# A two-block network on one core: filter spectra in four parts at four token norms, a second filter in the hyena output, two `w_out` pieces on VectorE, two `oa` chunks behind the inverse

## The reference, cut to what matters

```python
# once per layer; depends on the weights alone, not on the tokens
h = sin(freq[0] * (z @ fw1 + fb1)); h = sin(freq[1] * (h @ fw2 + fb2)); h = sin(freq[2] * (h @ fw3 + fb3))
h = (h @ fw4).reshape(L, 2, 512) * decay[:, None, :]
k = concat([h_fwd, 0, h_bwd[:0:-1]])
v_f, k_f = rfft(v, n=2 * L), rfft(k, n=2 * L)      # v depends on the tokens
y = irfft(v_f * k_f)[:, :L] + v * bias             # then times x0, then w_o_hyena
```

## Time and profile before

| | |
|---|---|
| runs of before, median of 3 | 2634.07 us (2632.21 to 2635.34) |
| the profiled execution | 2638.58 us, span 2636.6 us |
| PE matmul busy | 2520.5 us, 96% of the span |
| DVE, ACT, POOL busy | 43%, 48%, 55% |
| chain that ended last | PE 87%, ACT 5%, DVE 4%, issue 1%, POOL 1%, DMA 1% |
| mean granted TensorE clock | 0.986 |

### The profile page before, as it was taken

How to read it: one execution, slowest core, us unless ns; L and a number is a source line. 1 busy time by engine, 2 the same in 40 slices (tenths; PEclk the granted TensorE clock), 3 DMA queues, 4 the chain that set the end, 5 groups by cost and what they waited for, 6 DMA issues and landing times.

```text
span 2636.6 us, 42005 instructions
## 1 busy us (share of the span) xinstructions
PE 2520.5 (96%) x16564; PEld 2170.2 (82%) x16564; DVE 1131.5 (43%) x2158; ACT 1276.9 (48%) x2118; POOL 1440.5 (55%) x829
## 2 busy tenths in 40 slices
PE   6999999998999899999799999989999989999997
PEld 6998889988999789987577766766888868888997
DVE  7785545443976554534315512132101123525323
ACT  5457954355447964444544411342333345536543
POOL 5875746447976655444533122753555546463970
PEclk9999999999999999999899999999999999999999
DMA  5543343344543453343421111231222233234553
GB/s 217 191 161 145 128 160 145 130 178 173 191 161 144 144 177 112 144 152 141 160 80 65 49 64 64 96 116 72 90 94 96 96 112 112 86 136 180 189 180 143
DMA packets 50551, 347.62 MB, mean 132 GB/s; under 512 B 5312, under 2 KB 8640, under 8 KB 8896
## 3 DMA queue, kind: packets, MB, share of 16 engines
q1 hardware_dynamic: 47840, 340.31, 35.6%
q10 hardware_dynamic: 2528, 4.72, 0.5%
HBM read 343.96 MB, written 1.05 MB: 131 GB/s over the span
## 4 chain that ended last, share of the span: by engine, by line
PE 87%; ACT 5%; DVE 4%; issue 1%; POOL 1%; DMA 1%; SPq 0%; ACTq 0%; POOLq 0%; DVEq 0%
PE pg L1873 22%; PE pg L1875 21%; PE pg L1874 21%; PE pg L1898 2%; PE ps L2166 2%; PE ps L2187 2%; PE ps L2185 1%; PE pg L1896 1%; ACT ring_hi L758 1%; PE ps L2324 1%; PE ps L2305 1%; PE ps L1996 1%; PE ps L2021 1%; DMA ring<-in_w_stream_dram 1%; PE ps L2015 1%
## 5 line engine op out<-in xcount | busy, mean ns | idle before, releaser
L649 POOL TENSOR_TENSOR ring_lo<-ring,ring_hi 128x1024 fp32r<-128x1024 f32 (+2 forms) x498 | 1154.7, 2333 | 768.3 <-ACT ring_hi L758 767.9
L1873 PE MATMUL pg<-HH,ring_hi 128*128 128x256 f32 (+1 forms) x3360 | 1084.4, 323 | 45.3 <-DVE HL L1322 16.0
L1874 PE MATMUL pg<-HH,ring_lo 128*128 128x256 f32 (+1 forms) x3360 | 1029.9, 307 | 0.0
L1875 PE MATMUL pg<-HL,ring_hi 128*128 128x256 f32 (+1 forms) x3104 | 957.3, 308 | 0.0
L1873 PEld LDWEIGHTS pg<-HH,ring_hi 128*128 128x128 f32 x3360 | 641.3, 191 | 132.3 <-issue 64.2
L1874 PEld LDWEIGHTS pg<-HH,ring_lo 128*128 128x128 f32 x3360 | 642.3, 191 | 45.6 <-issue 18.2
L1875 PEld LDWEIGHTS pg<-HL,ring_hi 128*128 128x128 f32 x3104 | 592.9, 191 | 30.6
L758 ACT ACTIVATE ring_hi<-ring 128x1024 fp32r<-128x1024 f32 (+6 forms) x564 | 555.1, 1002 | 36.3 <-DMA ring<-in_w_stream_dram 35.4
L768 ACT ACTIVATE take<-pg 128x256 f32<-128x256 f32 (+1 forms) x260 | 110.9, 426 | 506.3 <-PE pg L1875 457.1
L1875 PE MATMUL pg<-big_r,ring_hi 128*128 128x256 f32 (+1 forms) x864 | 274.7, 318 | 0.0
L1873 PE MATMUL pg<-big_r,ring_hi 128*128 128x256 f32 (+1 forms) x736 | 240.3, 326 | 7.1 <-DVE big_r L1810 3.1
(11 more groups left out here) (327 smaller groups left out, 3214.5 us busy)
## 6 DMA issues: line engine op xcount, KB each, us to landing
ring<-in_w_stream_dram SPq DMA_DIRECT2D x320, 1024.0 KB, 4.8
hn<-in_consts_dram ACTq DMA_DIRECT2D x2, 1024.0 KB, 5.7
cst<-in_consts_dram SPq DMA_DIRECT2D x1, 1472.0 KB, 19.8
prm<-in_params_dram SPq DMA_DIRECT2D x1, 1110.0 KB, 7.4
X<-in_xT_dram SPq DMA_DIRECT2D x1, 1024.0 KB, 5.8
X<-in_ctxT_dram ACTq DMA_DIRECT2D x1, 1024.0 KB, 6.5
out_dram<-H ACTq DMA_DIRECT2D x1, 1024.0 KB, 4.8
cst<-in_consts_dram SPq DMA_DIRECT2D x1, 768.0 KB, 16.7
```

The source lines that it names most:

```text
L649: pool.tensor_tensor(ring_lo[:, slot, cols], ring[:, slot, cols], ring_hi[:, place * P:(place + n) * P].bitcast(F32), SUB).then_inc(sem(LO ...
L1873: first = pe.matmul(out, a[0], b[0], start=start, stop=False)
L1874: pe.matmul(out, a[1], b[0], start=False, stop=False)
L1875: return first, pe.matmul(out, a[0], b[1], start=False, stop=stop)
```

## The change

The spectrum is cut into four parts of 4 matmuls (8 instructions) each, every one into one bank: 2 or 3 of `ps`. Layer 0's parts stand at norms 2 and 3, layer 1's at norms 4 and 5: one part before the wait for the norm's sum (in place of the half `mod` chunk, which moves behind the sum with the other half), one part after the `mod` chunk. ACT copies the parts out two and two: parts 0 and 1 of layer 0 behind the squares of norm 3, all others behind the modulation (`modulate`) that follows. On DVE, layer 1's sine arguments and decay stand before the low parts of `mg2` 0, 1, 3 and 4; on PE, its steps stand behind `oh` 1, 4, 7 and 10. Layer 1's steps 0 to 3 move from the feed-forward into layer 0's `oh` chunks, with their table loads. The piece of `w_out` 1 goes to DVE and out of the hold. One turn (`modt`) moves one chunk later. In layer 1, two `oa` chunks move behind the inverse transform.

```diff
-    return gates[:2] + [row] + gates[2:3] + [turn] + gates[3:]
+    return gates[:2] + [row] + gates[2:4] + [turn] + gates[4:]
...
-    return spread([("oa", l, i) for i in range(2 * KD)], 5 if l == 0 else 3)
+    outs = [("oa", l, i) for i in range(2 * KD)]
+    return spread(outs, 5) + [[]] if l == 0 else spread(outs[:-2], 3) + [outs[-2:]]
...
-    if name == "w_out" and i == 0:
+    if name == "w_out" and i < 2:
         return True
...
-            need = [piece[4] for piece in PIECES if piece[8] <= last + (group[0][0] == "d_out")]
+            need = [piece[4] for piece in PIECES if piece[8] <= last + 2 * (group[0][0] == "d_out")]
...
+        KF_BANKS = (2, 3)
+        SPECTRA = {2: ([(0, 0)], [(0, 1)]), 3: ([(0, 2)], [(0, 3)]), 4: ([(1, 0)], [(1, 1)]), 5: ([(1, 2)], [(1, 3)])}
...
-        FILTER_1 = [6, 12, 3, 9, 13]
-        FILTER_2 = [0, 1, 2, 3, 4]
+        FILTER_1 = [6, 12, 3, 9]
+        FILTER_2 = [1, 4, 7, 10]
+        DECAY_AT = [0, 1, 3, 4]
...
+            def filter_spectrum(l, parts):
+                for ft in parts:
+                    act.wait_ge(sem("kf_ready"), 4 * l + ft + 1)
+                    act.activation(KFT[:, ft, :], ps[:, KF_BANKS[ft % 2], :], ACT.Copy).then_inc(sem("kf_done"), 1)
...
             for m in range(KD):
                 norm_square(3, m)
+            filter_spectrum(0, (0, 1))
             drain_fill(norm_mods(2, "turns"))
             norm_root(3)
...
                 modulate(mix_norm[l], l, 0)
+                filter_spectrum(l, (2, 3))
...
                 for i in range(2 * KD):
+                    if l == 0 and i - 2 in FILTER_2[:3]:
+                        ahead(CHUNK["oh", l, i])
+                        filter_sin(1, FILTER_2.index(i - 2))
                     drain_fill([("oh", l, i)])
+                    if l == 0 and i == 0:
+                        act.wait_ge(sem("hyena"), N_SEQ[0])
+                        act.dma_start(W4[0:64, :], fw4[1]).then_inc(sem("w4_loaded"), 16)
+                        act.dma_start(hn[:, :], consts[:, N_KEPT:]).then_inc(sem("filter_tables"), 16)
...
                 modulate(ffn_norm[l], l, 1)
                 if l == 0:
-                    act.wait_ge(sem("hyena"), N_SEQ[0])
-                    act.dma_start(W4[0:64, :], fw4[1]).then_inc(sem("w4_loaded"), 16)
-                    act.dma_start(hn[:, :], consts[:, N_KEPT:]).then_inc(sem("filter_tables"), 16)
+                    filter_spectrum(1, (0, 1))
...
+                    elif m in DECAY_AT[:3]:
+                        filter_argument(1, DECAY_AT.index(m))
+                    elif m == DECAY_AT[3]:
+                        filter_decay(1)
...
+            def filter_spectrum(l, ft):
+                bank = KF_BANKS[ft % 2]
+                if ft == 0:
                     pe.wait_ge(sem("h4_done"), l + 1)
+                if ft >= 2:
+                    pe.wait_ge(sem("kf_done"), 4 * l + ft - 1)
+                for q in range(4):
+                    ins = pe.matmul(ps[:, bank, :], table[...], VTK[:, q, :], start=q == 0, stop=q == 3)
+                ins.then_inc(sem("kf_ready"), 1)
...
             def norm(i):
-                fill(norm_mods(i, "before"))
+                if i in SPECTRA:
+                    for l, ft in SPECTRA[i][0]:
+                        filter_spectrum(l, ft)
+                else:
+                    fill(norm_mods(i, "before"))
                 pe.wait_ge(sem("norm_sum"), i + 1)
                 pe.matmul(ps[:, 0, 0:n], ones, rstd[:, 0:n], start=True, stop=True).then_inc(sem("norm_ss"), 1)
                 fill(norm_mods(i, "after"))
+                if i in SPECTRA:
+                    for l, ft in SPECTRA[i][1]:
+                        filter_spectrum(l, ft)
...
+                for i in range(1, 2 * KD):
+                    fill([("oh", l, i)])
+                    if l == 0 and i in FILTER_2:
+                        filter_step(1, FILTER_2.index(i))
```

More of the change, by code:

```diff
@@ L896, in filter_sin @@
                 act.activation(HQ[0:64, :], RR[0:64, 0, :], ACT.Sin).then_inc(sem("f_sin"), 1)
-            def filter_spectrum(l):
-                act.wait_ge(sem("kf_ready"), l + 1)
-                act.activation(KFT, ps[:, :, :], ACT.Copy).then_inc(sem("kf_done"), 1)
+            def filter_spectrum(l, parts):
+                for ft in parts:
+                    act.wait_ge(sem("kf_ready"), 4 * l + ft + 1)
+                    act.activation(KFT[:, ft, :], ps[:, KF_BANKS[ft % 2], :], ACT.Copy).then_inc(sem("kf_done"), 1)
             def attention_exp(l, it):
@@ L1094, in _ @@
                         filter_sin(0, 1 if m == 0 else 2)
-                    if l == DEPTH - 1 and m == KD - 1:
-                        merged_high(m - 1)
-                        ahead(CHUNK["d_out", l, 2 * m + 1])
-                        filter_spectrum(0)
                     drain_fill([("d_out", l, 2 * m + 1)])
-                    if 0 < m < KD - 1 or m and l < DEPTH - 1:
+                    if m:
                         merged_high(m - 1)
@@ L1184, in _ @@
                 drain_fill(next(gaps))
-                for s in range(ns):
-                    drain_fill(next(gaps))
-                    if s < ns - 1:
-                        drain_fill(next(gaps))
+                for items in gaps:
+                    drain_fill(items)
                 def merged2_high(m):
@@ L1211, in _ @@
                     drain(CHUNK["gu", l, 2 * i], AF[l][:, i % per, :], ACT.Silu, n)
-                    if l == 0 and i in FILTER_2[1:4]:
-                        filter_sin(1, FILTER_2.index(i) - 1)
                     to_take("gu", l, 2 * i + 1, n=n)
@@ L1218, in _ @@
                         hidden_high(i - 1)
-                    if l == 0 and i == FILTER_2[4] + 1:
-                        filter_spectrum(1)
                     if i % per == per - 1:
@@ L1793, in _ @@
                     dve.wait_ge(sem("vf_ready"), k + 1)
-                    dve.wait_ge(sem("kf_done"), l + 1)
+                    dve.wait_ge(sem("kf_done"), 4 * (l + 1))
                     dve.tensor_tensor(YFT[:, re, :], VFT[:, re, :], KFT[:, re, :], MUL)
@@ L1821, in _ @@
                     modulation(1, 0)
-                    for k in range(3):
-                        filter_argument(1, k)
-                    filter_decay(1)
                 for i in range(KF):
@@ L1976, in filter_step @@
                             pe.wait_ge(sem("hn_done"), HN_BASE1(1) + DO_N + 1)
-                        else:
-                            pe.wait_ge(sem("norm_rms"), ffn_norm[0] + 1)
                     else:
@@ L1982, in filter_step @@
                     pe.matmul(ps[0:64, 1, 0:T], lhsT, rhs, start=True, stop=True).then_inc(sem("f_ready"), 1)
-                elif step == 3:
+                else:
                     pe.wait_ge(sem("f_sin"), 3 * l + 3)
@@ L1990, in filter_step @@
                     ins.then_inc(sem("h4_ready"), 1)
-                else:
+            def filter_spectrum(l, ft):
+                bank = KF_BANKS[ft % 2]
+                if ft == 0:
                     pe.wait_ge(sem("h4_done"), l + 1)
-                    for ft in range(4):
-                        for q in range(4):
-                            table = C("dft_fwd") if q < 2 else DFT_BWD
-                            ins = pe.matmul(ps[:, ft, :], table[:, (q % 2) * N_FFT + ft * P:(q % 2) * N_FFT + (ft + 1) * P], VTK[:, q, :], start=q == 0, stop=q == 3)
-                    ins.then_inc(sem("kf_ready"), 1)
+                if ft >= 2:
+                    pe.wait_ge(sem("kf_done"), 4 * l + ft - 1)
+                for q in range(4):
+                    table = C("dft_fwd") if q < 2 else DFT_BWD
+                    ins = pe.matmul(ps[:, bank, :], table[:, (q % 2) * N_FFT + ft * P:(q % 2) * N_FFT + (ft + 1) * P], VTK[:, q, :], start=q == 0, stop=q == 3)
+                ins.then_inc(sem("kf_ready"), 1)
             def parts_of(high, low, n):
@@ L2408, in _ @@
                     ins.then_inc(sem("yi_ready"), 1)
+                fill(next(gaps))
                 fill([("oh", l, 0)])
                 pe.wait_ge(sem("hyena"), 2 * l + ns)
-                fill([("oh", l, i) for i in range(1, 2 * KD)])
+                for i in range(1, 2 * KD):
+                    fill([("oh", l, i)])
+                    if l == 0 and i in FILTER_2:
+                        filter_step(1, FILTER_2.index(i))
                 for m in range(KD):
@@ L2420, in _ @@
                         fill(norm_mods(ffn_norm[l], "turns"))
-                    if l == 0 and i in FILTER_2:
-                        filter_step(1, FILTER_2.index(i))
                     if i % per == per - 1:
```

## The result

The changed kernel takes 2598.74 us (median of 4 runs, 2596.97 to 2600.61), the kernel before 2634.70 in the same comparison (4 runs): ratio 0.9862, 95% interval 0.9849 to 0.9874. That is 36.0 us less; the forecast was 39.9 less and 2594.2, with a range of 2586 to 2604. The profiled execution took 2600.61 us, its span 2598.4, 38.2 less than that of before, so the terms can be measured almost in full against it.

The account below looks back on a forecast made before the run. PE bounds the kernel, busy for 2520.5 of 2636.6 us. Terms -20.3, -8.0, +9.1, -14.4, -4.65 and -1.65 sum to -39.9, taking the median from 2634.07 to 2594.2 us, range 2586 to 2604.

Parts of the forecast that it names:

- Term 1: Layer 1's `d_out` chunks: layer 0's spectrum leaves them, removing the time between `d_out` 13 and 15; -20.3 us.
- the 3.9 of the decay: Layer 1's `d_out` 15: the gain would be 3.9 us less only if PE had to wait for something else.
- Term 2: `w_out` 1 on DVE, both layers: POOL wait and half clock go, POOL late 0.5 at the end; -8.0 us.
- Term 3: Norms 2 and 3: layer 0's parts delay load 187, holding ACT before norm 3's root; +9.1 (E: `w_out` 7's end).
- Term 4: Layer 1's filter: steps cost nothing more in `oh`, spectrum parts fill idle time at norms 4 and 5; -14.4 us.
- so `gu` 0 comes 0.7 earlier; at norm 5 I take 0.3: Norms 4 and 5: a faster sum's matmul at full clock starts the following chunks earlier; -1.0 us in all.
- Term 5: Layer 1, two `oa` chunks behind the inverse: `oh` 1's wait and its half clock go; -4.65 us.
- Term 6: Turn one chunk later, both layers: its 0.95 us wait goes; between 0 and -3.3, middle taken, -1.65 us.
- (a): Norm 3: ACT is not held by load 187, that term is +1.7, time 2586.8 us; chance 0.1.
- (b): Clock does not recover at `w_out`, turn, `oh` 1, part 2: gives back 8.45 us, 2602.6 us; chance 0.2.
- (c): Norms 4 and 5: parts push the norm instead of hiding, 13.4 us come back, 2607.6 us; chance 0.05.
- (d): Ahead of `k2` 0: 7 us idle leaves PE at 1.2 GHz into layer 0's projections, slower than before; chance 0.02.

Follow-up runs that it names:

- F: Changed kernel with layer 0's spectrum whole again behind layer 1's `d_out` 13, half `mod` rows at norms 2 and 3: 2610.94 us, ratio 0.9907.
- D: Changed kernel with `w_out` 1 back on POOL and in the hold, both layers: 2606.60 us, ratio 0.9895.
- A: Changed kernel with ACT taking `q2` 0's weight piece behind the root of norm 3 instead of ahead of it: 2595.66 us, ratio 0.9855.
- B: Changed kernel with half of norm 3's `mod` row back ahead of part 2 and the sum: 2595.11 us, ratio 0.9854.
- G: Changed kernel with ACT loading the logarithm and exponential table early, ahead of the drains before a norm: 2598.51 us, ratio 0.9865.
- E: Changed kernel with layer 1's two `oa` chunks back ahead of the inverse: 2603.71 us, ratio 0.9881.
- C: Changed kernel with the turn back at its old place in both layers: 2598.81 us, ratio 0.9867.
- after: The changed kernel itself, against the kernel before: 2598.74 us, ratio 0.9862; run and profiled once more: 2599.93 us, ratio 0.9862.
- J: H with `q2` 0's piece taken behind the modulation of norm 3, not inside it: 2590.91 us, ratio 0.9829.
- I: G with the second chunk's piece taken inside the modulation at norms 1 and 6, not ahead of the root: 2598.83 us, ratio 0.9860.
- H: Changed kernel with the edits of A and G, and part 0 copied ahead of norm 3's squares: 2595.61 us, ratio 0.9853.

## Why the prediction was right, and where its sizes were off

The sign, the order of the terms and the mechanism of each held. The median lies 4.5 us above the forecast. 1.9 of it is the profiled execution (2600.61 for 2598.7), almost all in the terms (-38.2 for -39.9). The other 2.6 are the step from one execution to the median: the one profiled of before lay 4.5 above its median, by which the forecast was lowered, that of after only 1.9.

- **Term 1** (-20.3): -20.6 in the trace, and F gives it back. Right, the 3.9 of the decay with it: PE had nothing else to wait for.
- **Term 2** (-8.0): -7.6, D gives 7.5. The two parts were off against each other. The wait went as forecast, and the 0.5 of lateness which POOL was to run up over the steps did not come: PE is busy throughout `w_out` 1 to 7. But the half clock was worth 1.4 and 1.0 us, which is what the 3.76 and 3.82 leave over the waits of 2.39 and 2.81, not 1.7 each.
- **Term 3** (+9.1, 8.7 to 9.3): +8.37. The chain is the forecast one at each link: 1.02 idle before part 2, the `mod` row at E+15.8 (E+16.1), the load issued at E+17.0 (E+17.3), ACT's third piece at E+21.95 (E+22.1 to 22.7), DVE at E+24.27 (24.6 to 25.2). What is left is 0.3 at the start of the row and a landing of 4.9, the short end of the range. The fit of the Trainium skill, "DMA: Bandwidth & Descriptors", section "Anatomy of one DMA", that the prediction names beside this term is given there for transfers that GpSimd issues. These loads are issued by SP, and this one took 4.9 us, not 4.4. That its +8.3 lies so close to the measured +8.37 is luck: with the row's real start at E+15.8 it would have given +7.9. A and B show that it is this hold and that most of the term was to be had, in the traces 4.8 and 5.7 us of it.
- **Term 4** (-14.4): -13.6. The steps cost the same in both places (6.13 there), ACT's copies and the arguments hid, and the parts fitted the idle times. The step that failed is "so `gu` 0 comes 0.7 earlier; at norm 5 I take 0.3". The forecast took the sum's matmul for what released the root. It was ACT's own order: two pieces and a table load of 1.28, which ended 0.7 after even the slow matmul of before. The row for it was in the trace of before and was not read. G shows the 1.2 us behind it. The sums themselves came 0.1 later at each norm.
- **Term 5** (-4.65): -4.99, E gives 4.7 to 5.0. Right.
- **Term 6** (-1.65 between 0 and -3.3): -0.4 in the account above, and C, its undoing, does not move the median; by C against A it is worth 0 and 0.9. The row of the account for layer 1 hides some of that: it also holds norm 1, where after ran 6.8 us at half clock and before 3.4. The end near zero was the right one: in layer 0 the wait of 1.14 for POOL took the place of that for ACT, and the half clock stood behind it as before. That a stretch comes again "and nothing is won" was priced in; giving the middle was not reading, where POOL had the piece ready only 2.4 us behind the turn.
- **Not forecast**: +0.6 behind norm 6, where half clock lasted 6.8 us instead of 3.4. The second profile of after has 3.4 there and +0.1, so this differs between profiles of one kernel and is no effect of the change.

Of the rivals, (a) was what A, B and J then made; the trace of after refutes it for the change itself. (b), the clock, holds in part: half clock stayed behind both turns, went at `w_out` 1 and `oh` 1, and did not come at part 2. The Trainium skill, "TensorE: Matmul & The Clock Gate", section "A second HAM failure mode: psum-queue depth-cycling", tells of short idle times between groups of matmuls that keep the clock swinging; the trace agrees at the turns (0.50 behind waits of 1.14 and 0.42) and disagrees at part 2, where the clock stayed at 1.00 behind a wait of 1.02. At `w_out` 1 and `oh` 1 no wait was left that could show it. (c) came to 0.2 us instead of 13.4. (d) did not come: 6.8 us at half clock, from 1276.6 on, cover the end of that idle time and the first of `k2` 0, which DVE paces.

## What to carry to other kernels

When a wait is named for one releaser, read the row in front of the released instruction on its own engine too: if that row ends where it starts, the engine's order is the bound, and a faster releaser gives nothing. ACT takes its instructions in their order here, and so the root paid the 7.33 us for which the piece in front of it waited. A step that frees a slot for a load should be followed to the instruction that the loads hold, and either the issue or the order can be moved. A gain that is taken at one norm may not exist at the next, which has another last releaser: the early table gave 1.2 us at each of two norms and nothing at two others, and cost 1.4 and 1.2 in the two `w_out` groups, so that nothing was left of it.

## What the hardware showed that I had not expected

POOL's low part of a weight piece (2.4 us) keeps DVE's low part of the activations from ending: 0.71 us in after at norm 1, 2.13 in G, 2.07 in I, 2.21 for a pair in A and 2.20 in H, against 0.41 and 0.87 where POOL does nothing. In after, 18 of DVE's 88 low parts behind norms and in the merges start while an instruction of POOL runs: all 18 end 0.28 us behind that instruction, and the other 70 take 0.41 to 0.48. The product with an input in `ps` runs at its usual 0.48 beside POOL. Such a low part shows no idle time in front of it, only a long duration, so the list of waits does not show it. The Trainium skill, "SBUF — State Buffer", section "Who interferes with whom", says that a VectorE instruction with two inputs in SBUF contends with a GpSimd instruction that reads SBUF, and that the one issued second blocks fully. The trace agrees: in each of these cases POOL's instruction had begun first, and DVE's did not end before it.

The stretches at half clock stand behind idle times, short ones among them, but not behind each. Near 48 us, ahead of every edit, 6 of the 13 profiles of after and its variants have one and 7 do not; behind layer 1's turn 9 have one, at waits for POOL of 0.4 to 2.0 us, and 4 have none, at 0.3 to 0.6. Two profiles of after agree with each other up to 1188 us. So one profile against another differs by a few such stretches, each worth 1.0 to 1.6 us where PE has work throughout, whatever the edit, and for edits of this size the account by stretches said more than the medians. What decides it stays open.
